# Delta rule: the block-diagonal 128x128 matrices held as packed 64-wide chunks, their products done as 64x64 pairs

## The chip, the core and the metric

One core of a Trainium2 chip runs the whole program. The metric is the device time of one execution in microseconds, the median over several runs.

## What is computed

The program is two transformer blocks over one sequence of 1024 tokens, width 1024: a first block (sparse attention beside a convolution, then an MLP) and a second one (a pooling mixer beside a gated delta rule, then an MLP). The change is in the delta rule of the second block alone. It has 4 heads of 128 channels, chunks of 64 tokens, all in fp32:

```python
diff = gcum[..., :, None] - gcum[..., None, :]
decay_incl = jnp.exp(jnp.where(incl, diff, -jnp.inf))
decay_strict = jnp.where(strict, decay_incl, 0.0)
kb = kh * beta[..., None]
m = jnp.einsum('bhncd,bhnjd->bhncj', kb, kh) * decay_strict       # 64 x 64 per chunk
lhs = jnp.eye(C, dtype=f32) + m
rhs = jnp.concatenate([vh * beta[..., None], kb * jnp.exp(gcum)[..., None]], axis=-1)
sol = lax.linalg.triangular_solve(lhs, rhs, left_side=True, lower=True)
value, k_cumdecay = sol[..., :Dh], sol[..., Dh:]
attn_inner = jnp.einsum('bhncd,bhnjd->bhncj', qh, kh) * decay_incl
...
def step(state, inp):                                             # 16 chunks, one after another
    qd, kc, val, ai, kd, gl = inp
    v_new = val - jnp.einsum('bhcd,bhde->bhce', kc, state)
    o = jnp.einsum('bhcd,bhde->bhce', qd, state) + jnp.einsum('bhcj,bhje->bhce', ai, v_new)
    state = state * jnp.exp(gl)[..., None, None] + jnp.einsum('bhcd,bhce->bhde', kd, v_new)
    return state, o
```

## The kernel before, in words

The delta rule works on 8 tiles of 128 tokens, each two chunks of 64, with the four heads side by side: a matrix per head is 128x128, so a tensor of four is 128 partitions by 512 fp32, one PSUM bank. The matrices that belong to a chunk (m, the inverse of 1 + m, the inner attention) are block-diagonal: two 64x64 blocks in opposite corners, the other two corners zero by the masks `tri`, `strict` and `level[i]`.

The triangular solve is done by doubling. From m, level i's mask cuts out the part b_i that joins blocks of 2^i tokens. t is the inverse so far and u its transpose; level l computes z = b_l-transposed times u, then t - (product of z and t) and u - (product of t and z), l = 1 to 5, where the last needs u alone. Per tile: z1 to z5, t1 to t4, u1 to u5, fourteen groups of four products (one per head). Each fp32 product is two MATMUL instructions of PE, so a group is eight.

Every engine walks one list, `GSTEPS` (line 339), in order. `G_ORDER` gives the steps of a slot: finish_a, chunk_a (0), head_a, level_z 1 to 5, tail_a, chunk_b (0), finish_b, level_tu 1 to 5, chunk_a (1), finish_c, tail_b, head_b, chunk_b (1), head_z. A tile enters every three slots (`SETS = 3`, three sets of buffers `prep[t % 3]`, and PSUM banks 2 * set and 2 * set + 1, called x0 and x1), its step j runs in its slot j, so that three tiles at different depths share each slot. What each step does, with the lines of the profile:

- head_z: VectorE writes z = tri * g (L1798; L1790 for tile 0). head_a: PE multiplies ones by z (L2339, two instructions of 512 columns) into x0 and the gram product of kc with itself into x1 (L2325, the helper `heads`, whose line all group products have); VectorE df (L1801) and the two clamps (L1803, L1804); ScalarE three exponentials (L1200, L1202, L1203); POOL masks e2 (L790).
- head_b: PE kq (L2325); VectorE m from gram, beta and e1 (L1809, four instructions), ait (L1816), u0 (L1818); POOL b0 (L793), t (L795), b1 (L796), qdec (L799); PE turns b0 over (L2330, four transposes).
- level_z and level_tu: PE L2325, ScalarE copies z out of PSUM (L1206), VectorE subtracts t (L1824) and u (L1825), POOL prepares the next b (L808).
- tail_a, tail_b: PE turns kc and vc over, VectorE kbe, kd, vb (L1828, L1831, L1833), PE val and kct (L2325), ScalarE copies them out (L1211, L1213).
- chunk_a, chunk_b: the scan. PE kct and qdec with the state (L2377, L2380), VectorE vnew (L1842) and the decayed state (L1843), PE kd with vnew (L2386), VectorE the new state (L1848), and after the second chunk PE ait with vnew (L2390).
- finish_a to c: ScalarE ot (L1216), VectorE squares and sum, ScalarE root with a table load (L1219), VectorE rec, on and the gated product (L1856, L1858, L1862).

Semaphores `prep_mm`, `prep_dve`, `prep_act` and `prep_pool` count each tile's steps. POOL makes the masks (tri, strict, level) ahead of the list and, after it, splits the weights of the output product. The delta rule begins when the last input product of the second block is done and ends with the copies of h_lo (L1869) for that output product.

Two stretches of the first block are also read below: L2019, `pair_mm`, products of two heads whose operands lie in partitions 0 to 63 and 64 to 127, output to different banks; and L2097, products of 64 output rows that go in turn to PSUM partitions 0 to 63 and 64 to 127 of one bank:

```python
for e in range(2):
    row = slice(HD * e, HD * (e + 1))
    last = mm(ps[:, b[e] + c0 // HALF, 0:cn], q[e][l][row], r[row, c0:c0 + cn], start=(m == 0), stop=(m == 2))
...
last = mm(ps[h % 2 * HD:(h % 2 + 1) * HD, 6, h // 2 * P:(h // 2 + 1) * P],
          vtok[:, bb, kv * HD:(kv + 1) * HD], probT[:, e, bb, :], start=(bb == 0), stop=(bb == t))
```

Of the kernel before, what the change touches and what calls it, by code (L numbers as in the profile page):

```python
# [6 lines left out]
ALU = mybir.AluOpType  # L7
ACT = mybir.ActivationFunctionType
# [60 lines left out]
def build(nc, a, out):  # L69
    with ExitStack() as ctx:  # L70
# [150 lines left out]
        for i, base in enumerate((AH, AH + 32 * K1, AWHI)):  # L221
            names = ["e1", "e2", "egb", "m", "b0", "b1", "z", "t", "u", "kbe", "vb", "ait", "kd", "val", "kct", "qdec"]
            prep.append({nm: at(f"{nm}_{i}", [P, GH, P], F32, base + j * 2 * K1)
                         for j, nm in enumerate(names)})

# [148 lines left out]
        def hb(mask):  # L374

            return mask.unsqueeze(1).to_broadcast([P, GH, P])

# [202 lines left out]
        def _(pool):  # L580
# [204 lines left out]
            g.memset(state, 0.0).then_inc(sem("masks_ready"), 1)  # L785
            for kind, t, l in GSTEPS:
                b = prep[t % SETS]
                if kind == "head_a":
                    pool.wait_ge(prep_sem("act", t), prep_count("act", t, "e2"))
                    g.tensor_tensor(b["e2"], b["e2"], hb(tri), ALU.mult).then_inc(prep_sem("pool", t), 1)  # L790
                if kind == "head_b":
                    pool.wait_ge(prep_sem("dve", t), prep_count("dve", t, "m"))
                    g.tensor_tensor(b["b0"], b["m"], hb(level[0]), ALU.mult).then_inc(prep_sem("pool", t), 1)  # L793
                    pool.wait_ge(prep_sem("pool", t), prep_count("pool", t, "b0"))
                    g.tensor_tensor(b["t"], hb(ident), b["b0"], ALU.subtract).then_inc(prep_sem("pool", t), 1)  # L795
                    g.tensor_tensor(b["b1"], b["m"], hb(level[1]), ALU.mult).then_inc(prep_sem("pool", t), 1)  # L796
                    if t >= SETS:
                        pool.wait_ge(sem("scan_mm"), scan_count("mm", t - SETS, "kq1"))
                    g.tensor_tensor(b["qdec"], qc[:, :, t * P:(t + 1) * P], b["egb"],  # L799
                                    ALU.mult).then_inc(prep_sem("pool", t), 1)  # L800
                if kind == "level_z" and l < 5:

                    if l == 1:
                        pool.wait_ge(prep_sem("mm", t), prep_count("mm", t, "turn"))
                        pool.wait_ge(prep_sem("pool", t), prep_count("pool", t, "t0"))
                    else:
                        pool.wait_ge(prep_sem("mm", t), prep_count("mm", t, f"z{l - 1}"))
                    g.tensor_tensor(b[f"b{(l + 1) % 2}"], b["m"], hb(level[l + 1]), ALU.mult).then_inc(prep_sem("pool", t), 1)  # L808
# [8 lines left out]
        def _(act):  # L817
# [375 lines left out]
            for kind, t, l in GSTEPS:  # L1193
# [10 lines left out]
                if kind == "level_z":  # L1204
                    act.wait_ge(prep_sem("mm", t), prep_count("mm", t, f"z{l}"))
                    s.activation(b["z"], x0, ACT.Copy).then_inc(prep_sem("act", t), 1)  # L1206
# [40 lines left out]
        def _(dve):  # L1247
# [544 lines left out]
            for kind, t, l in GSTEPS:  # L1792
# [12 lines left out]
                if kind == "head_b":  # L1805
                    dve.wait_ge(prep_sem("mm", t), prep_count("mm", t, "gram"))
                    dve.wait_ge(prep_sem("act", t), prep_count("act", t, "e1"))
                    for h in range(GH):
                        last = v.scalar_tensor_tensor(b["m"][:, h, :], x1[:, h, :], gs["beta"][:, t, h:h + 1],  # L1809
                                                      b["e1"][:, h, :], ALU.mult, ALU.mult)  # L1810
# [5 lines left out]
                    v.tensor_tensor(b["ait"], x0, b["e2"], ALU.mult).then_inc(prep_sem("dve", t), 1)  # L1816
                    dve.wait_ge(prep_sem("mm", t), prep_count("mm", t, "turn"))
                    v.tensor_tensor(b["u"], hb(ident), x1, ALU.subtract).then_inc(prep_sem("dve", t), 1)  # L1818
                if kind == "level_tu":
                    dve.wait_ge(prep_sem("mm", t), prep_count("mm", t, f"u{l}"))  # L1820
                    if l < 5:
                        if l == 1:
                            dve.wait_ge(prep_sem("pool", t), prep_count("pool", t, "t0"))
                        v.tensor_tensor(b["t"], b["t"], x0, ALU.subtract).then_inc(prep_sem("dve", t), 1)  # L1824
                    v.tensor_tensor(b["u"], b["u"], x1, ALU.subtract).then_inc(prep_sem("dve", t), 1)  # L1825
# [70 lines left out]
        def _(pe):  # L1896
# [420 lines left out]
            for kind, t, l in GSTEPS:  # L2317
# [9 lines left out]

                def turns(out, src):
# [4 lines left out]
                if kind == "head_a":  # L2333
# [88 lines left out]
```

## Time and profile before

| | us |
|---|---|
| median of 3 runs | 2888.5 (2883.8 to 2890.9) |
| the profiled execution, its own time | 2888.1 |
| its span | 2886.3 |
| busy: PE 93%, VectorE (DVE) 58%, POOL 40%, ScalarE (ACT) 26% | 2687.2, 1686.2, 1153.8, 763.3 |
| mean granted TensorE clock | 0.975 |

PE is TensorE's matmuls, PEld its weight loads. A line of the chain of waits tells where the time that ended last was spent; "x16" after it counts the instructions merged. A line of a timeline has the start, the time from the first start to the last end of the merged instructions, and in brackets the idle time before and what ended it.

### The profile page before, as it was taken

What the parts mean: (1) busy time and instruction counts of PE and PEld (TensorE: products, weight loads), DVE (VectorE), ACT (ScalarE), POOL (GpSimd) and SP (SyncE); (2) the same over time, 40 slices, a digit from 0 to 9 for tenths busy, and PEclk for the clock granted to TensorE, in tenths of its full rate; (3) what the DMA queues carried; (4) which work ended last, traced back from release to release, by engine and by line L of the source; (5) the groups of instructions that cost most, each with busy time, mean ns of one, the idle gap of its engine ahead of it and who ended that gap; (6) DMA issues with size and microseconds to landing.
All of it is one profiled execution on the core that took longest, in us unless ns stands there. A gap on an engine that the chain in (4) does not pass through costs nothing.

```text
span 2886.3 us, 34827 instructions
## 1 busy us (share of the span) xinstructions
PE 2687.2 (93%) x13584; PEld 2207.5 (76%) x13584; DVE 1686.2 (58%) x2150; ACT 763.3 (26%) x1322; POOL 1153.8 (40%) x764
## 2 busy tenths in 40 slices
PE   4999888989999999999999998788799999999998
PEld 4867766777788888888876677777688888888887
DVE  6278988764766567566585772455526334444335
ACT  4235467544321000111032431222214100111002
POOL 2422464544545335345342223333264334334332
PEclk8999999999999999999999999899999999999999
DMA  6201132012311111111122110000221111111111
GB/s 218 66 12 34 38 102 66 8 38 77 106 59 58 38 51 55 40 51 52 43 70 73 37 37 15 1 1 1 93 90 58 42 46 58 39 48 58 36 51 59
DMA packets 142490, 153.35 MB, mean 53 GB/s; under 512 B 7183, under 2 KB 105252, under 8 KB 142374
## 3 DMA queue, kind: packets, MB, share of 16 engines
q1 hardware_dynamic: 137088, 143.97, 15.7%
q10 hardware_dynamic: 5286, 7.79, 0.8%
q8 instruction: 78, 1.28, 0.2%
q14 instruction: 38, 0.31, 0.0%
HBM read 143.35 MB, written 8.39 MB: 53 GB/s over the span
## 4 chain that ended last, share of the span: by engine, by line
PE 77%; DVE 13%; ACT 5%; issue 4%; DMA 1%; POOL 1%; ACTq 0%; SPq 0%; DVEq 0%; POOLq 0%
PE ps L1943 11%; PE ps L1944 11%; PE ps L1928 11%; PE ps L1945 11%; PE ps L1930 11%; PE ps L1929 11%; PE ps L2325 4%; ACT sel_out L960 2%; DVE yt L1765 2%; PE ps L2019 1%; DVE score L1398 1%; DVE yt L1754 1%; DVE best L1396 1%; PE ps L2097 1%; PE ps L1911 1%
## 5 line engine op out<-in xcount | busy, mean ns | idle before, releaser
L1928 PE MATMUL ps<-h_hi,w_hi 128*128 128x512 f32 x1472 | 585.6, 398 | 10.1 <-issue 5.6
L1929 PE MATMUL ps<-h_lo,w_hi 128*128 128x512 f32 x1472 | 575.3, 391 | 0.0
L1930 PE MATMUL ps<-h_hi,w_lo 128*128 128x512 f32 x1472 | 575.1, 391 | 0.0
L707 POOL TENSOR_TENSOR w_hi<-raw,zero 128x1024 fp32r<-128x1024 f32 x128 | 243.7, 1904 | 781.3 <-PE ps L1930 398.4
L1943 PE MATMUL ps<-w_hi,u_hi 128*128 128x512 f32 x1024 | 399.3, 390 | 0.0
L1945 PE MATMUL ps<-w_hi,u_lo 128*128 128x512 f32 x1024 | 399.1, 390 | 0.0
L1944 PE MATMUL ps<-w_lo,u_hi 128*128 128x512 f32 x1024 | 399.1, 390 | 0.0
L1089 ACT ACTIVATE act_r<-ps 128x512 f32<-128x512 f32 x128 | 76.4, 597 | 1131.9 <-PE ps L1930 1131.9
L1649 DVE TENSOR_TENSOR act_r<-act_r 128x512 f32<-128x512 f32 x128 | 165.3, 1292 | 331.0 <-ACT act_r L1089 331.0
L710 POOL TENSOR_TENSOR w_lo<-raw,w_hi 128x1024 fp32r<-128x1024 f32 x128 | 338.1, 2642 | 10.1
L1928 PEld LDWEIGHTS ps<-h_hi,w_hi 128*128 128x128 f32 x1472 | 278.0, 189 | 77.3 <-issue 17.3
L1929 PEld LDWEIGHTS ps<-h_lo,w_hi 128*128 128x128 f32 x1472 | 278.2, 189 | 59.9 <-issue 3.7
L1930 PEld LDWEIGHTS ps<-h_hi,w_lo 128*128 128x128 f32 x1472 | 277.8, 189 | 58.6
L1654 DVE TENSOR_TENSOR u_lo<-act_r,u_hi 128x512 fp32r<-128x512 f32 x128 | 226.8, 1782 | 0.0
L1943 PEld LDWEIGHTS ps<-w_hi,u_hi 128*128 128x128 f32 x1024 | 192.8, 188 | 40.1
L1944 PEld LDWEIGHTS ps<-w_lo,u_hi 128*128 128x128 f32 x1024 | 192.8, 188 | 40.0
L1945 PEld LDWEIGHTS ps<-w_hi,u_lo 128*128 128x128 f32 x1024 | 192.7, 188 | 40.0
L1662 DVE TENSOR_TENSOR x<-x,ps 128x512 f32<-128x512 f32 x128 | 88.0, 687 | 212.2 <-PE ps L1945 212.2
L1943 PE MATMUL ps<-w_hi,h_hi 128*128 128x512 f32 (+2 forms) x512 | 184.3, 360 | 18.3 <-DVE h_lo L1869 6.8
L1944 PE MATMUL ps<-w_lo,h_hi 128*128 128x512 f32 (+2 forms) x512 | 182.5, 357 | 0.0
L1945 PE MATMUL ps<-w_hi,h_lo 128*128 128x512 f32 (+2 forms) x512 | 182.1, 356 | 0.0
L1669 DVE TENSOR_TENSOR x<-x,tmp 128x512 f32<-128x512 f32 x128 | 155.0, 1211 | 4.4
(421 smaller groups left out, 4163.9 us busy)
## 6 DMA issues: line engine op xcount, KB each, us to landing
raw<-in_w_up_dram SPq DMA_DIRECT2D x64, 512.0 KB, 4.0
raw<-in_w_down_dram SPq DMA_DIRECT2D x64, 512.0 KB, 3.2
raw<-in_w_ada_dram SPq DMA_DIRECT2D x48, 512.0 KB, 3.7
raw<-in_w_in_dram SPq DMA_DIRECT2D x32, 512.0 KB, 3.7
raw<-in_w_out_dram SPq DMA_DIRECT2D x32, 512.0 KB, 3.2
x<-in_x_dram SPq DMA_DIRECT2D x12, 512.0 KB, 9.4
x_mid<-x SPq DMA_DIRECT2D x8, 512.0 KB, 5.4
x<-x_mid ACTq DMA_DIRECT2D x8, 512.0 KB, 7.4
```

What stands on the lines that cost most here:

```text
L707: g_.tensor_tensor(w_hi[:, r, :], raw[:, r, :], zero.to_broadcast([P, 1024]), ALU.add).then_inc(sem("w_hi_done"), 1)
L710: g_.tensor_tensor(w_lo[:, r, :], raw[:, r, :], w_hi[:, r, :].bitcast(F32), ALU.subtract).then_inc(sem("split_done"), 1)
L1649: v.tensor_tensor(act_r[:, b % 4, :], act_r[:, b % 4, :], act_r[:, b % 4, :], ALU.mult).then_inc(sem(f"u_sq{k}"), 1)
L1654: v.tensor_tensor(u_lo[c // 4][:, c % 4, :], act_r[:, c % 4, :], u_hi[c // 4][:, c % 4, :].bitcast(F32), ALU.subtract).then_inc(sem(f"u_lo ...
L1669: v.tensor_tensor(x[:, t, cols], x[:, t, cols], tmp2[:, n % 2, :], ALU.add).then_inc(sem(f"x_sum{k}"), 1)
L1928: mm(ps[:, bank, :], wh, h_hi[:, k, cols], start=(k == 0), stop=False)
L1929: mm(ps[:, bank, :], wh, h_lo[:, k, cols], start=False, stop=False)
L1930: last = mm(ps[:, bank, :], wl, h_hi[:, k, cols], start=False, stop=(k == NK - 1))
L1943: mm(o, hi[:, k0 + k, tok], wh, start=(start and k == 0), stop=False)
L1944: mm(o, hi[:, k0 + k, tok], wl, start=False, stop=False)
L1945: last = mm(o, lo[:, k0 + k, tok], wh, start=False, stop=(stop and k == 1))
L2325: last = mm(out[:, h, :], lhs[:, h, :], rhs[:, h, :], start=True, stop=True)
```

## The change

The block-diagonal matrices are packed: e1, e2, m, b0, b1, t, u and z (as zp) become 128 partitions by 4 heads by 64 columns, the upper 64 partitions holding chunk 0's block and the lower ones chunk 1's. The masks get packed copies. gram and kq are made by `column_blocks`, per head two products with all 128 rows of contraction and 64 weight columns and 64 moving columns, whose outputs go to partitions 0 to 63 and 64 to 127 of one bank. z, t, u and the turn of b0 (now a product with the packed identity) are made by `blocks`, per head two 64x64x64 products, chunk 0 from partitions 0 to 63 to partitions 0 to 63 of bank 2 * set, chunk 1 from the other half to the other half of bank 2 * set + 1. Where such a result is read from PSUM it is read by two instructions, one per chunk. The last u (uf) and ait are written to full 128x128 form, whose zero corners POOL clears once per set. The turn now also waits for ait, and tail_a's first turn for u5.

```diff
@@ prep buffers
+            prep[-1]["uf"] = prep[-1]["e2"]
+            for nm, place in (("e1", slot["e1"]), ("e2", slot["e1"] + K1), ("m", slot["m"]), ("t", slot["t"]), ("u", slot["u"]),
+                              ("b0", slot["b0"]), ("b1", slot["b0"] + K1), ("zp", slot["z"])):
+                prep[-1][nm] = at(f"{nm}_half_{i}", [P, GH, CHUNK], F32, place)
+        maskp = at("maskp", [P, 8, CHUNK], F32, AH + 5 * 2 * K1)
+        identp = at("identp", [P, CHUNK], F32, AH + 7 * 2 * K1 + K1)
+        BLOCKS = [slice(CHUNK * c, CHUNK * (c + 1)) for c in range(2)]
+        def chunk_ps(set_, c, part):
+            r = BLOCKS[c]
+            return v3(ps[r, 2 * set_ + c, part * GH * CHUNK:(part + 1) * GH * CHUNK], GH)
+        def packed(b):
+            return v3(ps[:, b, 0:GH * CHUNK], GH)
@@ POOL
+            pool.wait_ge(sem("cm2_full"), cm2_need(len(CH2) - 1))
+            for r in BLOCKS:
+                g.tensor_copy(maskp[r], masks[r, :, r]).then_inc(sem("halves_ready"), 1)
+                g.tensor_copy(identp[r], ident[r, r]).then_inc(sem("halves_ready"), 1)
+            pool.wait_ge(sem("halves_ready"), 4)
...
+                    if t < SETS:
+                        g.memset(b["ait"], 0.0).then_inc(sem("halves_ready"), 1)
+                        g.memset(b["uf"], 0.0).then_inc(sem("halves_ready"), 1)
-                    g.tensor_tensor(b["e2"], b["e2"], hb(tri), ALU.mult).then_inc(prep_sem("pool", t), 1)
+                    g.tensor_tensor(b["e2"], b["e2"], hp(trip), ALU.mult).then_inc(prep_sem("pool", t), 1)
...
@@ ScalarE
-                    s.activation(b["z"], x0, ACT.Copy).then_inc(prep_sem("act", t), 1)
+                    for c, r in enumerate(BLOCKS):
+                        last = s.activation(b["zp"][r], chunk_ps(t % SETS, c, 0), ACT.Copy)
+                    last.then_inc(prep_sem("act", t), 1)
@@ VectorE
-                    v.tensor_tensor(b["e1"], x0, tb(gs["gcum"][:, t, :]), ALU.subtract).then_inc(prep_sem("dve", t), 1)
+                    for r in BLOCKS:
+                        last = v.tensor_tensor(b["e1"][r], x0[r, :, r],
+                                               gs["gcum"][r, t, :].unsqueeze(2).to_broadcast([CHUNK, GH, CHUNK]), ALU.subtract)
...
-                    v.tensor_tensor(b["ait"], x0, b["e2"], ALU.mult).then_inc(prep_sem("dve", t), 1)
+                    dve.wait_ge(sem("halves_ready"), 4 + 2 * min(t + 1, SETS))
+                    for r in BLOCKS:
+                        last = v.tensor_tensor(b["ait"][r, :, r], packed(2 * (t % SETS))[r], b["e2"][r], ALU.mult)
...
-                    v.tensor_tensor(b["u"], hb(ident), x1, ALU.subtract).then_inc(prep_sem("dve", t), 1)
+                    for c, r in enumerate(BLOCKS):
+                        last = v.tensor_tensor(b["u"][r], hp(identp, r), chunk_ps(t % SETS, c, 1), ALU.subtract)
...
-                        v.tensor_tensor(b["t"], b["t"], x0, ALU.subtract).then_inc(prep_sem("dve", t), 1)
+                        for c, r in enumerate(BLOCKS):
+                            last = v.tensor_tensor(b["t"][r], b["t"][r], chunk_ps(t % SETS, c, 1), ALU.subtract)
+                    if l == 5 and t >= SETS:
+                        dve.wait_ge(prep_sem("mm", t - SETS), prep_count("mm", t - SETS, "kct"))
+                    for c, r in enumerate(BLOCKS):
+                        last = v.tensor_tensor(b["uf"][r, :, r] if l == 5 else b["u"][r], b["u"][r], chunk_ps(t % SETS, c, 0),
+                                               ALU.subtract)
@@ PE
+                def column_blocks(b, lhs, rhs, what):
+                    for h in range(GH):
+                        for r in BLOCKS:
+                            last = mm(packed(b)[r, h, :], lhs[:, h, r], rhs[:, h, r], start=True, stop=True)
+                    last.then_inc(prep_sem("mm", t), 1)
+                def blocks(part, lhs, rhs, what):
+                    for h in range(GH):
+                        for c, r in enumerate(BLOCKS):
+                            last = mm(chunk_ps(t % SETS, c, part)[:, h, :], lhs[r, h, :], rhs[r, h, :], start=True, stop=True)
+                    last.then_inc(prep_sem("mm", t), 1)
...
-                    heads(x1, kc[:, :, tok], kc[:, :, tok], "gram")
+                    column_blocks(n0 + 1, kc[:, :, tok], kc[:, :, tok], "gram")
...
-                    heads(x0, kc[:, :, tok], qc[:, :, tok], "kq")
+                    column_blocks(n0, kc[:, :, tok], qc[:, :, tok], "kq")
+                    pe.wait_ge(sem("halves_ready"), 4)
                     pe.wait_ge(prep_sem("pool", t), prep_count("pool", t, "b0"))
-                    turns(x1, b["b0"]).then_inc(prep_sem("mm", t), 1)
+                    pe.wait_ge(prep_sem("dve", t), prep_count("dve", t, "ait"))
+                    blocks(1, b["b0"], hp(identp), "turn")
...
-                    heads(x0, b[f"b{l % 2}"], b["u"], f"z{l}")
+                    blocks(0, b[f"b{l % 2}"], b["u"], f"z{l}")
...
-                        heads(x0, b["z"], b["t"], f"t{l}")
-                    heads(x1, b["t"], b["z"], f"u{l}")
+                        blocks(1, b["zp"], b["t"], f"t{l}")
+                    blocks(0, b["t"], b["zp"], f"u{l}")
                 if kind == "tail_a":
+                    pe.wait_ge(prep_sem("dve", t), prep_count("dve", t, "u5"))
                     turns(x0, kc[:, :, tok]).then_inc(prep_sem("mm", t), 1)
-                    pe.wait_ge(prep_sem("dve", t), prep_count("dve", t, "u5"))
                     turns(x1, vc[:, :, tok]).then_inc(prep_sem("mm", t), 1)
...
-                    heads(x1, b["u"], b["vb"], "val")
-                    heads(x0, b["kbe"], b["u"], "kct")
+                    heads(x1, b["uf"], b["vb"], "val")
+                    heads(x0, b["kbe"], b["uf"], "kct")
```

The other masked products of POOL (b0, t, b1 to b5) and VectorE's m take the packed operands and masks in the same way.

## Rows read from the trace of the kernel before

**Rows 1.** The page of the kernel before, its head.
```profile
span 2886.3 us, 34827 instructions
```

**Rows 2.** Chain that ended last, 1500 to 2200 us: start us, us, what.
```profile
1793.55 2.09 PE ps L2325 x8
1796.31 3.79 PE ps L2325 x16
1801.56 2.06 PE ps L2325 x8
...
1810.15 2.05 PE ps L2339 x2
...
1839.61 1.14 PE ps L2339 x2
...
2006.59 1.51 PE ps L2339 x2
...
2084.17 1.30 DVE h_lo L1869 x2
```

**Rows 3.** The same chain within one steady period, 1937 to 1975 us.
```profile
1939.11 2.06 PE ps L2339 x2
...
1944.53 2.07 PE ps L2325 x16
...
1950.34 0.66 PE ps L2330 x4
1951.00 1.02 PE ps L2377 x8
...
1952.91 2.05 PE ps L2325 x16
...
1956.05 3.77 PE ps L2325 x32
...
1967.17 1.28 ACT L1219
...
1972.90 1.94 PE ps L2339 x2
```

**Rows 4.** Timeline of PE, 655 to 677 us: start us, us, line, xcount.
```profile
660.13 0.40 PE L2123 MATMUL ps<-glu_hi,diag_hi 128*128 128x512 f32 x1
660.36 0.39 PE L2124 MATMUL ps<-glu_lo,diag_hi 128*128 128x512 f32 x1
...
667.13 0.40 PE L2019 MATMUL ps<-k_lo,q_hi 64*128 64x512 f32 x2
667.37 0.39 PE L2019 MATMUL ps<-k_hi,q_lo 64*128 64x512 f32 x2
667.68 1.97 PE L2097 MATMUL ps<-probT,vtok 128*64 128x128 f32 x32
```

**Rows 5.** Timeline of PE's weight loads, 654.3 to 656.2 us.
```profile
655.09 0.19 PEld L2019 LDWEIGHTS ps<-k_hi,q_hi 64*128 64x128 f32 x2
```

**Rows 6.** Groups by line and form, 1785 to 2085 us.
```profile
L1825 DVE TENSOR_TENSOR u<-u,ps 128x512 f32<-128x512 f32 x40 | 26.6, 680 | 0.0
L1206 ACT ACTIVATE z<-ps 128x512 f32<-128x512 f32 x40 | 23.8, 595 | 75.6 <-PE ps L2325 75.6
...
L793 POOL TENSOR_TENSOR b<-m,masks 128x512 f32<-128x512 f32 x8 | 10.1, 1264 | 18.2 <-DVE m L1809 18.2
...
L1809 DVE SCALAR_TENSOR_TENSOR m<-ps,g_beta,e 128x128 f32<-128x128 f32 x32 | 9.0, 344 | 0.8 <-ACT e L1202 0.8
...
L1759 DVE TENSOR_TENSOR zc<-ps,zc 128x1024 f32<-128x1024 f32 x1 | 1.2, 1225 | 0.3 <-ACT zc L1168 0.3
```

**Rows 7.** Stretches: us; busy PE, PEld, DVE, ACT, POOL; PEclk; DMA share, GB/s.
```profile
1805.00:1810.10 5.10, 3.07 (x15) 2.78 (x14) 1.89 (x3) 0.00 (x0) 0.00 (x0) 0.50 0.00 0
1969.30:1972.90 3.60, 0.66 (x4) 0.45 (x5) 3.45 (x6) 0.76 (x1) 0.00 (x0) 1.00 0.00 0
1972.90:1975.00 2.10, 2.10 (x4) 1.06 (x5) 0.12 (x1) 0.00 (x0) 0.00 (x0) 0.53 0.00 0
```

More of the change, by code:

```diff
@@ L224, in build @@
                          for j, nm in enumerate(names)})
+            slot = {nm: base + j * 2 * K1 for j, nm in enumerate(names)}
+            prep[-1]["uf"] = prep[-1]["e2"]
[4 more added lines that the diff above has]
+        identp = at("identp", [P, CHUNK], F32, AH + 7 * 2 * K1 + K1)
+        trip, levelp = maskp[:, 0, :], [maskp[:, 2 + i, :] for i in range(6)]
+        BLOCKS = [slice(CHUNK * c, CHUNK * (c + 1)) for c in range(2)]
         ps = nc.alloc_psum_tensor("ps", [P, 8, HALF], F32).ap()
@@ L376, in hb, with hp @@
             return mask.unsqueeze(1).to_broadcast([P, GH, P])
+        def hp(mask, rows=slice(0, P)):
+            return mask[rows].unsqueeze(1).to_broadcast([rows.stop - rows.start, GH, CHUNK])
+        def chunk_ps(set_, c, part):
[3 more added lines that the diff above has]
+            return v3(ps[:, b, 0:GH * CHUNK], GH)
         def tb(col):
@@ L807, in _ @@
                         pool.wait_ge(prep_sem("mm", t), prep_count("mm", t, f"z{l - 1}"))
-                    g.tensor_tensor(b[f"b{(l + 1) % 2}"], b["m"], hb(level[l + 1]), ALU.mult).then_inc(prep_sem("pool", t), 1)
+                    g.tensor_tensor(b[f"b{(l + 1) % 2}"], b["m"], hp(levelp[l + 1]), ALU.mult).then_inc(prep_sem("pool", t), 1)
             pool.wait_ge(sem("scan_mm"), scan_count("mm", LAST_AT_W, "ai"))
@@ L1800, in _ @@
                     dve.wait_ge(prep_sem("mm", t), prep_count("mm", t, "gb"))
-                    v.tensor_tensor(b["e1"], x0, tb(gs["gcum"][:, t, :]), ALU.subtract).then_inc(prep_sem("dve", t), 1)
+                    for r in BLOCKS:
+                        last = v.tensor_tensor(b["e1"][r], x0[r, :, r],
+                                               gs["gcum"][r, t, :].unsqueeze(2).to_broadcast([CHUNK, GH, CHUNK]), ALU.subtract)
+                    last.then_inc(prep_sem("dve", t), 1)
                     dve.wait_ge(prep_sem("dve", t), prep_count("dve", t, "df"))
@@ L1808, in _ @@
                     for h in range(GH):
-                        last = v.scalar_tensor_tensor(b["m"][:, h, :], x1[:, h, :], gs["beta"][:, t, h:h + 1],
+                        last = v.scalar_tensor_tensor(b["m"][:, h, :], packed(2 * (t % SETS) + 1)[:, h, :], gs["beta"][:, t, h:h + 1],
                                                       b["e1"][:, h, :], ALU.mult, ALU.mult)
@@ L1815, in _ @@
                         dve.wait_ge(sem("scan_mm"), scan_count("mm", t - SETS, "ai"))
-                    v.tensor_tensor(b["ait"], x0, b["e2"], ALU.mult).then_inc(prep_sem("dve", t), 1)
+                    dve.wait_ge(sem("halves_ready"), 4 + 2 * min(t + 1, SETS))
+                    for r in BLOCKS:
+                        last = v.tensor_tensor(b["ait"][r, :, r], packed(2 * (t % SETS))[r], b["e2"][r], ALU.mult)
+                    last.then_inc(prep_sem("dve", t), 1)
                     dve.wait_ge(prep_sem("mm", t), prep_count("mm", t, "turn"))
-                    v.tensor_tensor(b["u"], hb(ident), x1, ALU.subtract).then_inc(prep_sem("dve", t), 1)
+                    for c, r in enumerate(BLOCKS):
+                        last = v.tensor_tensor(b["u"][r], hp(identp, r), chunk_ps(t % SETS, c, 1), ALU.subtract)
+                    last.then_inc(prep_sem("dve", t), 1)
                 if kind == "level_tu":
@@ L1823, in _ @@
                             dve.wait_ge(prep_sem("pool", t), prep_count("pool", t, "t0"))
-                        v.tensor_tensor(b["t"], b["t"], x0, ALU.subtract).then_inc(prep_sem("dve", t), 1)
-                    v.tensor_tensor(b["u"], b["u"], x1, ALU.subtract).then_inc(prep_sem("dve", t), 1)
+                        for c, r in enumerate(BLOCKS):
+                            last = v.tensor_tensor(b["t"][r], b["t"][r], chunk_ps(t % SETS, c, 1), ALU.subtract)
+                        last.then_inc(prep_sem("dve", t), 1)
+                    if l == 5 and t >= SETS:
[3 more added lines that the diff above has]
+                                               ALU.subtract)
+                    last.then_inc(prep_sem("dve", t), 1)
                 if kind == "tail_a":
```

6 lines of the change are left out of this document (3 added, 3 removed).

## The prediction

> **What bounds the kernel now.** I began with the page's first part: the span is 2886.3 us [rows 1]. The change touches only the delta rule, so I looked for it in the chain of waits over 1500 to 2200 us. Eight tiles of 128 tokens enter one after another, each with the product of ones and z (L2339); the next phase begins with h_lo (L1869) at 2084.17 [rows 2]. The tiles' starts give the stages: fill, in which tile 0 and then tile 1 enter (1810.15), up to tile 2's start at 1839.61; five steady periods, 1839.61 to 2006.59, 33.4 us each; and the drain, 2006.59 to 2084.17, 77.6 us. Together that is a tenth of the kernel, and all that the change can gain is in there.
>
> In one steady period [rows 3], 33.8 us from 1939.11 to 1972.90, I see three parts. **A**, from L2339 to the turn of b0 at 1950.34 (11.2 us), goes through VectorE's and ScalarE's head work until t3, u3 start at 1944.53, 5.4 us in, and then through a queue of five products on TensorE. **B**, the turn to about 1964.7, is almost bare TensorE: the scan's products, z1 and z4 (x16, 2.05 us), then t1, u1, t4, u4 (x32, 3.77 us). **C**, to 1972.90, waits for ScalarE (table load and root at 1967.17) and then VectorE; TensorE hardly matters. So TensorE's product groups are worth their price in B, part of it in A, nearly nothing in C. From x16 in 2.05 and x32 in 3.77, 16 instructions cost 1.72 us, 0.11 us each: a group of four heads, eight instructions since each fp32 product is two, costs 0.88 us, and its result comes 0.2 us after its last start.
>
> **The change, part by part.**
>
> *The products.* gram, kq and turn, five z, four t and five u become 64x64 halves: 16 instructions a group in place of eight (the turn's were four). Whether it pays hangs on the rate. Four bounds: (1) A matmul with 64 rows of contraction alternating between the two row halves: the second product costs nothing. Pairs of 64x512 start 0.24 us apart (667.13 and 667.37) and single 128x512 ones 0.23 us (660.13, 660.36) [rows 4]; their two weight loads run side by side too, x2 in 0.19 us [rows 5]. (2) Outputs alternating between column halves: L2097, 64 weight columns and 128 moving ones, x32 in 1.97 us, 0.055 us each [rows 4], half of the 0.11 us of full products. (3) With the moving columns halved as well, 0.055 becomes 0.0275 us: a group costs 0.44 us. (4) The other end is 0.055 us, the fastest rate of weight load plus matmul that a row shows: 0.88 us, no gain at all. For the products in opposite corners (turn, z, t, u) I take 0.44, since rows 4 and 5 show both matmuls and loads of different row halves together; for gram and kq, whose pairs share all rows, I take L2097's rate, 0.88.
>
> *Changes of shape.* From one form to another there is a small gap: L2019's last pair starts at 667.37 and L2097 only at 667.68, 0.31 us later in place of 0.23 [rows 4]. I take 0.09 us a change, about eight more of them a period, half on the path; between 0 and 0.15.
>
> *Packed element work.* A VectorE operation from PSUM takes 1225 ns at 1024 elements and 680 at 512 [rows 6]: 1.06 ns an element, so 256 take 0.41 us, and the second of two, whose fixed part overlaps, starts about 0.33 later (no less than the 0.27 of its elements). Where a copy is split by chunk (df, ait, u0, t, u) two halves take about 0.75 in place of 0.68: +0.07 each. They can't be under half of 0.68 nor over twice it. ScalarE's z, 595 ns, becomes two halves of 0.39, 0.32 apart: +0.1. Operations truly halved gain: two clamps and two exponentials -0.13 to -0.2 each, m (four of 344 ns) -0.25, POOL's products 1264 ns to about 0.73 (between 0.63 and 1.26).
>
> *Part A.* df +0.07, clamps -0.26, the ScalarE run e1, e2, z3 -0.3: t3 starts at 4.9 in place of 5.4 (if none of the halves is cheaper than the whole, at 5.4 again). Then on TensorE t3 and u3 0.88, change 0.09, val and kct 1.76, change 0.09, kq 0.88, result 0.2: 8.8. Here the added wait bites: the turn now waits for ait, which needs kq; queued behind the turn stand chunk_a, z1 and z4. ait's halves end at 9.55, the turn starts at 9.6 (11.2 before). The other leg, t3/u3 on VectorE (1.4), m (0.85), b0 (0.8), ends at 9.0, so ait is late next. A gains 1.6 us.
>
> *Part B.* The turn 0.66 becomes 0.44 and a change; chunk_a keeps its 1.9; z1 and z4 2.05 become 0.97: -1.0. t1, u1, t4, u4 3.77 become 1.76 and 0.2: -1.8. The rest (chunk_a, its vnew wait, kdv, ai) stays. ScalarE's z4 is ready just when t4 comes. B gains 2.9.
>
> *Part C.* z2 and z5 come 0.4 to 0.5 sooner, t2, u2, u5 are six halves: +0.2. The table load, root, rec, on, gated and z stay. C gains 0.3. tail_a's kc turn now waits for u5 of its tile, which VectorE finished in the part before: nothing.
>
> *Sum.* 4.8 us off 33.8 is 29.0 a period. The 33.8 holds a slow start: TensorE's granted clock is 0.53 right after the idle stretch (1972.9 to 1975.0) [rows 7], 1.2 instead of 2.4 GHz, while the period that begins at 1839.61 has L2339 in 1.14 us [rows 2]. With longer idle in C I expect that in all: 5 x (33.4 - 29.0) = 22. *Fill*: tile 0 runs alone, and at half clock: one level took 1801.56 - 1793.55 = 8.0 us [rows 2], z 2.09 and t, u 3.79 of it. Halved products leave 1.1 and 2.0, the split copies cost 0.2: 2.7 a level, two levels 5.4, and 2.4 in tile 0's head (POOL's masking of e2 and b0, then t and b1 against the turn, 1.7; clamps and exponentials 0.7): 7.8. Tile 1's 29.5 us hold three slots of the same kind, partly at full clock: 7, between 4 and 9. *Drain*: one period's 4.8, then 1.35 and 1.2 where z, t, u are still in the way of chunk_a: 7.3; the last 20 us are scan alone, nothing. *POOL's new copies* of the masks and memsets sit between the last input product and e2's mask, under L2339 and VectorE's head: nothing; uncovered they cost up to 2 us once. Total 22 + 7.8 + 7 + 7.3 = 44 us. The profiled execution took 2888.1 us, 1.8 around its span and 0.4 below the median of 2888.5. 2888.1 - 44 = 2844.
>
> **Rivals.** *1. Halves do not overlap, or issue limits them:* 0.055 us each, a group 0.88, the turn dearer by 0.3. For it: no row shows a weight load and matmul pair under 0.055 us. Against: rows 5. Then A gains 0.8 and loses 0.3 at the turn, changes and split copies take the rest, the fill keeps 2: about 2885, from 2881 to 2890. Chance 0.20. The Trainium skill, page "TensorE: Matmul & The Clock Gate", section "Wait — 56ns, not 53.3ns?", says that the sequencer, without hardware decode, spends about 62 ns on each matmul, which binds once array work is shorter. By it a group would be 0.99 us and the time some 8 us above this rival's. L2097's 32 in a row at 55 ns speak against it, but no run shows narrower ones; of the 0.20, 0.03 is for it.
>
> *2. The clock stays low; the slower end.* TensorE's work a period falls from 25 to about 18 us and its idle share grows. Rows 7 show both sides: from 1805 to 1810 busy for 3.07 of 5.10 us the clock stayed at 0.50, while it was 1.00 in 1969.3 to 1972.9 after a dense stretch, with 0.66 busy of 3.6, and fell right after. Place: parts A and B. Price: at 1.2 GHz A costs 3.6 us more (t3, u3, val, kct, kq), B 9.5, C 0.5: 13.6 a period, 42.6 in place of 29.0. Over five periods, less fill and drain, that is about 2915. It decides against the change once more than a third of each period (4.8 of 13.6) is at 1.2 GHz. Against: B is dense in the new schedule too, and density has lifted the clock. Chance 0.10, two thirds of it slower than before.
>
> *3. More gain:* kq overlaps too, the changes of shape are free and the low start shrinks: another 1 to 2 us a period and 4 in the fill, 2830. Chance 0.10.
>
> **How the numbers follow.** Forecast 0.60, with its own range 2832 to 2866 (group price 0.40 to 0.60, fill 4 to 9). Measured no-change for this kernel is about 0.3%, 8.7 us. Faster: 0.60, 0.10, part of rival 2 (0.03) and of rival 1 (0.04): 0.77. Same: most of rival 1, 0.15. Slower: 0.07 of rival 2 and the rest of rival 1: 0.08. The range reaches 2824 (rival 3 and a cheaper fill) to 2882, leaving out most of rivals 1 and 2.
>
> **What would show it.** L2339's starts about 29 us apart; t, u, z groups x16 in about 0.6 us; the chain in B still TensorE; the turn released by ait; tile 1's start to tile 2's about 22 us. Groups at 0.9 to 1.0 us show rival 1; granted clock 0.5 in B shows rival 2. I am wrong if the periods stay at 33 with short groups: then a wait that I took as covered has the place of the products.

## The result, and the profile after

The changed kernel takes 2871.95 us, the median of 4 runs (2870.19 to 2875.62), against 2889.08 us for the kernel before in the same comparison: 0.9945 of it, 95% interval 0.9928 to 0.9963. It is faster by 17 us. The forecast was 2844 us, 44 us less than the profiled execution, with a range of 2824 to 2882.

The page of the kernel after, its head:

```profile
span 2868.5 us, 37231 instructions
...
PE 2649.3 (92%) x14704; PEld 2162.1 (75%) x14704; DVE 1699.3 (59%) x2246; ACT 766.0 (27%) x1362; POOL 1125.3 (39%) x774
```

The span is 17.8 us shorter than that of [rows 1], though TensorE has 1120 matmuls more. The product of ones and z, with which each tile starts, is now L2397, and the 64x64 products are L2383. The chain of waits over 1750 to 2100 us (start us, us, what) has the tiles' starts and the fill:

```profile
1784.93 1.11 PE ps L2397 x2
...
1791.94 0.86 PE ps L2383 x16
1793.65 2.00 PE ps L2383 x32
1797.55 1.13 PE ps L2383 x16
...
1804.14 2.06 PE ps L2397 x2
...
1828.85 1.12 PE ps L2397 x2
...
1989.93 1.70 PE ps L2397 x2
...
2065.31 1.30 DVE h_lo L1915 x2
```

Beside [rows 2]: in the kernel before tile 0 started here:

```profile
1784.33 1.10 PE L2339 MATMUL ps<-z,ones 128*128 128x512 f32 x2 [0.98 <-DVE z L1790]
```

The delta rule, from tile 0's product of ones and z to h_lo, took 2084.17 - 1784.33 = 299.8 us and takes 2065.31 - 1784.93 = 280.4 us, so 19.4 us went here. What the three stages gave, in us:

| | before | forecast | after |
|---|---|---|---|
| fill, tile 0's start to tile 2's | 55.3 | 40.5 | 43.9 |
| five periods, us each | 33.4 | 29.0 | 32.2 |
| drain, tile 7's start to h_lo | 77.6 | 70.3 | 75.4 |

The loss against the forecast is above all in the steady periods: 22 us were expected of them and 6 came. The chain within one of them, 1957.24 to 1989.93, to be laid beside [rows 3]:

```profile
1957.24 2.05 PE ps L2397 x2
...
1962.47 0.69 DVE kbe L1874
...
1964.42 2.05 PE ps L2371 x16
1966.47 0.64 PE ps L2377 x16
...
1968.13 0.68 PE ps L2383 x16
...
1970.71 1.08 PE ps L2383 x32
...
1972.87 1.10 PE ps L2383 x32
...
1974.00 0.41 DVE t_half L1864
...
1974.42 0.42 DVE t_half L1864
...
1974.88 0.41 DVE u_half L1869
...
1975.31 0.42 DVE u_half L1869
...
1977.49 0.62 DVE vnew L1888
...
1980.61 1.93 PE ps L2383 x32
...
1983.34 1.28 ACT L1250
...
1985.79 0.41 DVE t_half L1864
...
1989.93 1.70 PE ps L2397 x2
```

The lines to see are the pairs of L1864 and L1869. After the products of the four groups (x32, 1.10 us at the end, in place of the 3.77 us of [rows 3]) the chain no longer goes on with chunk_a on TensorE. It goes through eight halves on VectorE, from 1974.00 until vnew at 1977.49, and through six more before the next tile, from 1985.79. A half is 0.41 us long and the next starts 0.42 to 0.46 us after it: no overlap at all. The second thing is the start of the period. kbe begins 5.2 us after L2397, and val and kct (L2371) start only when vb is done, 7.2 us after it. The clock there and in part C, by the same columns as [rows 7]:

```profile
1957.20:1962.40 5.20, 5.16 (x39) 3.45 (x40) 1.43 (x4) 1.97 (x5) 0.73 (x2) 0.50 0.01 3
1979.90:1983.40 3.50, 3.49 (x53) 3.08 (x53) 1.51 (x3) 2.16 (x6) 0.00 (x0) 0.52 0.00 0
```

The first 5.2 us of the period are at 0.50, and z2 and z5 in part C (0.52) are at the low clock too, x32 in 1.93 us. Before, the first stretch (1939.1 to 1944.3) had 0.69. Not every period is like this one. Over the five, the starts of L2397 are 32.1, 31.1, 32.0, 33.2 and 32.7 us apart; z2 and z5 are at the low clock in the first, fourth and fifth, and take 1.15 us in the other two. The mean granted clock of the five is 0.88, against 0.97 before.

Groups by line and form over 1785 to 2070 us, to be read beside [rows 6]:

```profile
L2383 PE MATMUL ps<-u_half,b_half 64*64 64x64 f32 x640 | 30.8, 257 | 7.1 <-DVE u_half L1869 5.1 <-DVE u_half L1856 2.1
...
L2383 PE MATMUL ps<-identp,b_half 64*64 64x64 f32 x128 | 5.5, 222 | 10.8 <-DVE ait L1852 8.2 <-POOL b_half L822 2.5
```

The 640 instructions of the z groups have 257 ns each in flight, against 299 for the full products before; what fell is the distance between them, for in the chain above two groups, 32 instructions, last 1.08 us. The turn (identp, b_half) waited 10.8 us in all over eight tiles, 8.2 of them for ait.

### The profile page after: what moved, and what is told of

Read it like the earlier page. It is cut to its first block, busy times and chain, and to the rows that moved or that the text cites. A ratio compares the mean times of both kernels' runs of the same rounds, so it can differ in the third digit from the quotient of the medians.

```text
span 2868.5 us, 37231 instructions
## 1 busy us (share of the span) xinstructions
PE 2649.3 (92%) x14704; PEld 2162.1 (75%) x14704; DVE 1699.3 (59%) x2246; ACT 766.0 (27%) x1362; POOL 1125.3 (39%) x774
## 4 chain that ended last, share of the span: by engine, by line
PE 76%; DVE 14%; ACT 5%; issue 4%; DMA 1%; POOL 0%; ACTq 0%; SPq 0%; DVEq 0%; POOLq 0%
PE ps L1989 11%; PE ps L1991 11%; PE ps L1990 11%; PE ps L1974 11%; PE ps L1976 11%; PE ps L1975 11%; ACT sel_out L989 2%; PE ps L2383 2%; DVE yt L1796 2%; PE ps L2065 2%; DVE score L1429 1%; DVE yt L1785 1%; DVE best L1427 1%; PE ps L2143 1%; DVE u_half L1869 1%
## 5 line engine op out<-in xcount | busy, mean ns | idle before, releaser
L1974 PE MATMUL ps<-h_hi,w_hi 128*128 128x512 f32 x1472 | 585.5, 398 | 10.1 <-issue 5.6
L731 POOL TENSOR_TENSOR w_lo<-raw,w_hi 128x1024 fp32r<-128x1024 f32 x128 | 338.1, 2642 | 10.1
```

The lines of the kernel that those rows point to most:

```text
L731: g_.tensor_tensor(w_lo[:, r, :], raw[:, r, :], w_hi[:, r, :].bitcast(F32), ALU.subtract).then_inc(sem("split_done"), 1)
L1974: mm(ps[:, bank, :], wh, h_hi[:, k, cols], start=(k == 0), stop=False)
```

## The experiments

Times below are medians of four or more runs. The kernel before was run again in each comparison, with medians of 2887.3 to 2890.2 us, and each ratio is to its own. "Stretch" is tile 0's start to h_lo in the profiled execution; tile 0 starts anywhere from 1782.75 to 1787.48 us in these executions, so stretches and periods are compared beside the medians.

| kernel | us | ratio to before, interval | stretch | period |
|---|---|---|---|---|
| before | 2889 | | 299.8 | 33.4 |
| after | 2872.0 | 0.9945 (0.9928 to 0.9963) | 280.4 | 32.2 |
| whole_reads | 2843.7 | 0.9833 (0.9816 to 0.9849) | 258.4 | 29.0 |
| chunk_order | 2866.6 | 0.9911 (0.9894 to 0.9927) | 276.8 | 30.9 |
| warm_clock | 2866.9 | 0.9922 (0.9906 to 0.9939) | 276.7 | 31.0 |
| no_pairs | 2894.3 | 1.0014 (1.0004 to 1.0024) | 303.0 | 33.7 |
| whole_warm | 2844.4 | 0.9851 (0.9834 to 0.9867) | 256.5 | 28.2 |
| whole_early_z | 2818.2 | 0.9760 (0.9744 to 0.9776) | 228.6 | 25.2 |
| before_early_z | 2871.7 | 0.9951 (0.9934 to 0.9968) | 282.7 | 30.7 |
| one_bank | 2842.8 | 0.9844 (0.9828 to 0.9861) | 256.7 | 29.0 |
| whole_short_warm | 2841.0 | 0.9829 (0.9812 to 0.9845) | 249.5 | 27.5 |
| best_no_ait_wait | 2813.2 | 0.9732 (0.9715 to 0.9748) | 224.8 | 24.0 |

**whole_reads: one suspected cost taken away.** The theory after the first look: the split reads on VectorE took back what the products gave. The rival: the clock did.

```diff
+        ORDER = [(0, 0), (2, 1), (1, 0), (3, 1), (0, 1), (2, 0), (1, 1), (3, 0)]
+        def head_ps(set_, h, c, part):      # heads 0, 1 in the first bank, 2, 3 in the second
+            col = part * GH * CHUNK + h % 2 * CHUNK
+            return ps[BLOCKS[c], 2 * set_ + h // 2, col:col + CHUNK]
-                            last = v.tensor_tensor(b["t"][r], b["t"][r], chunk_ps(t % SETS, c, 1), ALU.subtract)
+                        v.tensor_tensor(two(b["t"]), two(b["t"]), whole(t % SETS, 1), ALU.subtract)
```

> The changed kernel with the chunks' results laid out so that VectorE and ScalarE read them whole: heads 0 and 1 of both chunks in the first bank of the set, heads 2 and 3 in the second, order of the pairs such that the two at work write different banks. z, u0, t and u up to level 4 are then one instruction of 128x256 each in place of two of 64x256. Theory (the split reads ate the gain: two halves follow each other 0.43 us apart, so t1, u1, t4, u4 take 3.5 us on the path, t2, u2, u5 2.6 us): consecutive whole ones 0.33 us apart, t1, u1, t4, u4 in 1.5 us, a steady period 3 us shorter (29 in place of 32.2), 2846 us in all, 2840 to 2855. Rival (the low clock is what ate it): the period shortens by less than 1 us, 2864 to 2872. Rival (TensorE is slower with banks shared by the two chunks): x16 groups above 0.7 us.

Measured: 2843.7 us, a period of 29.0. The timeline of VectorE in part B, and one line of TensorE in part C:

```profile
1952.62 0.42 DVE L1873 TENSOR_TENSOR t_half<-t_half,ps 128x256 f32<-128x256 f32 x1 [0.41 <-PE ps L2393]
...
1952.96 0.41 DVE L1877 TENSOR_TENSOR u_half<-u_half,ps 128x256 f32<-128x256 f32 x1
...
1953.56 0.42 DVE L1873 TENSOR_TENSOR t_half<-t_half,ps 128x256 f32<-128x256 f32 x1 [0.18 <-PE ps L2393]
1953.90 0.41 DVE L1877 TENSOR_TENSOR u_half<-u_half,ps 128x256 f32<-128x256 f32 x1
...
1955.43 0.69 DVE L1898 TENSOR_TENSOR vnew<-val,ps 64x512 f32<-64x512 f32 x1 [1.12 <-PE ps L2450]
...
1958.35 1.15 PE L2393 MATMUL ps<-u_half,b_half 64*64 64x64 f32 x32
```

t and u are one instruction each, 0.34 us apart, and vnew starts at 1955.43, released by TensorE's chunk_a: part B is bare TensorE again. The last line is z2 and z5 in part C: x32 in 1.15 us, full clock, and so in all five periods. The theory holds in size, 28 us where 26 were expected, and both rivals fall as the main cause. ScalarE has a share in it: from the start of z2 to the table load of L1219's counterpart it is 1.60 us here (1958.35 to 1959.95) and 2.30 us in the kernel after where the clock is full (1883.17 to 1885.47), since four halves of z are copied in 1.56 us and two whole ones in 0.85.

**chunk_order: why halves are dear.** The same halves in another order.

```diff
                     for c, r in enumerate(BLOCKS):
-                        last = v.tensor_tensor(b["t"][r], b["t"][r], chunk_ps(t % SETS, c, 1), ALU.subtract)
-                    for c, r in enumerate(BLOCKS):
+                        if l < 5:
+                            last_t = v.tensor_tensor(b["t"][r], b["t"][r], chunk_ps(t % SETS, c, 1), ALU.subtract)
                         last = v.tensor_tensor(b["uf"][r, :, r] if l == 5 else b["u"][r], b["u"][r], chunk_ps(t % SETS, c, 0),
```

> The changed kernel with VectorE's halves of a level ordered t, u of chunk 0, then t, u of chunk 1, in place of t of both, u of both. Theory (two instructions lose their overlap when the first partition changes from 0 to 64 or back; with the same first partition they overlap by about 0.1 us, as vnew after u of the second chunk does): the four take 1.55 in place of 1.75 us, two of three starts change to one of three, a period 0.4 to 0.6 us shorter, 2868 us. Rival (short instructions cannot overlap, whatever their partitions): four still 1.75 us, 2872.

```profile
1968.92 0.41 DVE L1866 TENSOR_TENSOR t_half<-t_half,ps 64x256 f32<-64x256 f32 x1 [0.40 <-PE ps L2383]
1969.25 0.41 DVE L1869 TENSOR_TENSOR u_half<-u_half,ps 64x256 f32<-64x256 f32 x1
1969.67 0.42 DVE L1866 TENSOR_TENSOR t_half<-t_half,ps 64x256 f32<-64x256 f32 x1
1970.02 0.42 DVE L1869 TENSOR_TENSOR u_half<-u_half,ps 64x256 f32<-64x256 f32 x1
```

t and u of chunk 0 start 0.33 us apart, u of chunk 0 and t of chunk 1 0.42, then 0.35. So it isn't the shortness. Two instructions that start at the same partition overlap by 0.08 us; where the first partition changes, they don't. The Trainium skill, page "VectorE: DVE Perf Modes", section "Two Vector instructions with no wait between them", has this as a rule, which it calls a model: an instruction whose input or output starts in another group of 32 partitions than the last one in that memory is held until every earlier one has finished. The traces agree: held halves start 0.42 us after neighbours that are 0.41 long, and here every second one is free of it. By that rule every half of a period but the first of each run would have been priced at its full length ahead of the run, for each starts on other partitions than the one ahead of it. The kernel before had the sign of it too, in vnew and the decay of the state behind it. vnew of chunk 0 starts at partition 0 and that of chunk 1 at partition 64, the state always at 0:

```profile
1952.92 0.68 DVE L1842 TENSOR_TENSOR vnew<-val,ps 64x512 f32<-64x512 f32 x1 [1.20 <-PE ps L2380]
1953.53 1.10 DVE L1843 TENSOR_TENSOR state<-state,egb 128x512 f32<-128x512 f32 x1
...
1961.74 0.69 DVE L1842 TENSOR_TENSOR vnew<-val,ps 64x512 f32<-64x512 f32 x1 [0.61 <-PE ps L2380]
1962.46 0.69 DVE L1843 TENSOR_TENSOR state<-state,egb 128x512 f32<-128x512 f32 x1
```

The starts are 0.61 us apart for chunk 0 and 0.72 for chunk 1.

The median is 5.4 us less than after, where 4 were expected. A period is 1.3 us shorter, more than the 0.6 expected, and what is over goes with the clock: TensorE's wait for vnew1 (vnew of chunk 1) is 0.96 us here and 1.38 us in the kernel after, and z2 and z5 behind it are at the full clock in all five periods here, at the low one in three of five there. That the longer stall brings the clock down is suggested by this, not isolated.

**warm_clock: the other suspect.**

```diff
+                    pe.wait_ge(sem("scan_dve"), scan_count("dve", t, "snew1"))
+                    for i in range(6):
+                        mm(bank(6)[:, i % GH, :], ones, ident, start=True, stop=True)
                     pe.wait_ge(sem("scan_dve"), scan_count("dve", t, "on"))
                     turns(bank(7), ot).then_inc(sem("scan_mm"), 1)
+                    for i in range(14):
+                        mm(bank(6)[:, i % GH, :], ones, ident, start=True, stop=True)
```

> The changed kernel with idle products of ones and the identity added on TensorE into bank 6, which is free there: 6 before the wait for on, 14 after the turn of ot, about 4 us of work in the stretch in which TensorE waits for VectorE before each tile. Nothing of the result is changed. Theory (the granted clock falls in that stretch and part A then runs at 1.2 GHz up to kbe): granted clock 1.00 over the first 5 us of a period, L2339's counterpart 1.1 us in place of 2.05, kbe starts 3.2 us after it in place of 5.2, the period 1.5 to 2 us shorter, 2858 us, 2854 to 2864. Rival (part A is bound by the element work anyway): kbe sooner, val no sooner, 2870 to 2873.

```profile
1955.30:1960.50 5.20, 4.40 (x74) 3.25 (x74) 3.32 (x7) 1.97 (x5) 1.42 (x2) 1.00 0.00 0
```

The clock is 1.00 over the first 5.2 us, and a period is 31.0 in place of 32.2, 1.2 less where 1.5 to 2 were expected. The median fell by 5 us, not 14: it lies outside the expected 2854 to 2864, and the intervals of the two ratios overlap, so the gain is read from the stretch, 3.6 us shorter. Part A, from L2397 to the turn, is 8.9 us in place of 10.9, as the theory has it; but the wait for vnew1 is still there, z2 and z5 still run at the low clock in four of the five periods, part C is half a microsecond longer, and the drain 2.2 us. The clock is a real cost, but not the main one.

**no_pairs: does the overlap of corners exist?** One line swapped, `for c` outside `for h`.

> The changed kernel with the 64x64 products ordered by chunk: all four heads of chunk 0, then all of chunk 1, so that neighbours use the same corner of the array. Theory (pairs in opposite corners overlap, 0.028 us an instruction): a group x16 goes from 0.64 to about 1.05 us at full clock, the two z groups x32 from 1.08 to 1.9, a period 1.5 to 2.5 us longer, 2885 to 2892 us. Rival (the rate is set by something else than corners): unchanged, 2872.

The timeline of TensorE:

```profile
1965.57 1.54 PE L2383 MATMUL ps<-u_half,b_half 64*64 64x64 f32 x32
...
1985.59 0.93 PE L2383 MATMUL ps<-identp,b_half 64*64 64x64 f32 x16 [1.05 <-DVE ait L1852]
```

Two z groups last 1.54 us in place of 1.15, the turn 0.93 in place of 0.68. The expected 1.9 and 1.05 were too much, and so was the rate of rival 1 in the prediction, but the total, 2894.3, is beyond the expected 2885 to 2892: 22 us slower than after, and nothing of the change's gain is left. The pairs are what makes it pay.

**whole_warm and whole_short_warm: both costs at once.** The idle products on whole_reads, first with 14 after the turn, then with 8.

> Whole reads (as in whole_reads, 2843.7 us) and the idle products that keep TensorE's clock up before each tile (as in warm_clock, which took 1.5 us off a period of the changed kernel). If the two costs are separate: period 29.0 to 27.5, 2836 us, 2833 to 2840. If the split reads hid the clock's cost, or the other way round: 2842 to 2845.

> whole_warm with 8 idle products in place of 14 after the turn of ot, since the 14 stood on the chain of waits before the product of ones and z there. Theory (the clock costs 1.5 us a period also with whole reads): 27.3 to 27.9 us a period, 2836 us, 2833 to 2841. Rival: 28.5 to 29.0, 2842 to 2846.

whole_warm missed: 2844.4. Its chain of waits shows why:

```profile
1931.92 1.54 PE ps L2466 x12
...
1933.97 3.13 PE ps L2470 x28
1937.10 0.88 PE ps L2407 x2
```

With whole reads the idle stretch is 1 us shorter, and the 14 idle products (L2470, 3.13 us) stand on the chain ahead of L2407. With 8 a period is 27.5 us, 1.5 less than whole_reads, as the theory has it, and 2841.0 us is at the edge of the expected 2833 to 2841. The medians differ by only 2.7 us, although the stretch is 8.9 us shorter. In the two profiled executions tile 0 starts 4.0 us later and the time is 4.5 us less, which leaves 0.5 us lost behind h_lo; and the profiled execution of whole_reads was its slowest, 1.9 us above its median, that of this kernel 0.1 above. Why tile 0 starts later in one execution than in another is open.

**one_bank: is "each chunk in its own bank" needed?**

```diff
-            return ps[BLOCKS[c], 2 * set_ + h // 2, col:col + CHUNK]
+            return ps[BLOCKS[c], 2 * set_ + part, h * CHUNK:(h + 1) * CHUNK]
```

> Whole reads with all eight blocks of a group in one bank: chunk 0 in partitions 0 to 63, chunk 1 in partitions 64 to 127, pairs in the plain order, so that the two products at work write the same bank in different partitions. Theory (only the partitions matter): as whole_reads, x16 at 0.64 us, 2844 us, 2841 to 2847. Rival, a rule of the Trainium skill, page TensorEngine Tiling (Array Packing), Gotcha 1: row tiles cannot access one bank simultaneously; the pairs would be serial, x16 at 0.9 us or more, 2860 us or more.

```profile
1954.14 0.68 PE L2391 MATMUL ps<-t_half,zp_half 64*64 64x64 f32 x16
1954.65 0.63 PE L2391 MATMUL ps<-zp_half,t_half 64*64 64x64 f32 x16
```

The groups start 0.46 to 0.51 us apart, as in whole_reads, and the time is the same, though the pairs are back in the plain order: so it wasn't their order that helped in whole_reads. The rule of the Trainium skill, page "TensorEngine Tiling (Array Packing)", section "Gotcha 1: PSUM Pressure", that the expectation took as its rival doesn't hold here, for products in opposite corners, whose outputs lie in different partitions. So the layout of the change was not needed for the pairs, and it is what forced the reads to be split.

**whole_early_z, before_early_z: the chain of part C.** One entry of the list of steps moved, on whole_reads and on the kernel before.

```diff
-        G_ORDER += [("chunk_b", 7, 0), ("finish_b", 8, 0)]
+        G_ORDER += [("chunk_b", 7, 0), ("head_z", -1, 0), ("finish_b", 8, 0)]
```

> Whole reads, and head_z (z = tri * g, which needs only what is long there) moved in the order of steps from the end of the slot to before finish_b, where VectorE waits for ScalarE's table load and root. Theory (part C is a chain of VectorE: on, t, u, u5, gated, z, and then TensorE's product of ones and z): that product starts right after the turn of ot, df 2.3 us sooner, a period 29.0 to 26.8, 2828 us, 2823 to 2833. Rival (part A is bound elsewhere, by ktp and kbe): a period 28 to 29, 2838 to 2844.

> The kernel before with head_z moved in the same way and nothing else. Theory: part C is the same chain there, so it gains 2 us a period, 2874 us, 2870 to 2880: then the move is independent of the packed products. Rival (before, TensorE and not VectorE bounds the start of a tile): 2884 to 2890.

The chain is as the theory has it in both, and the size in the second: 16 us less than before (15 expected). A period of before_early_z is 30.7: this one moved entry is worth as much as the whole change. On whole_reads it gives 25 us where 16 were expected, and 2818.2 is below the expected 2823 to 2833. Part C is 6.85 us there in place of 9.26, near the 2.3 expected, and part A about 8.9 in place of 10.3, which the expectation didn't have. Granted clock over the five periods of whole_early_z, by the columns of [rows 7]:

```profile
1816.50:1942.30 125.80, 105.55 (x1793) 92.12 (x1791) 82.39 (x181) 38.88 (x70) 36.64 (x45) 1.00 0.01 2
```

With L2407's counterpart right after the turn of ot, TensorE's long idle stretch is gone, and with it the fall of the clock, which whole_short_warm had priced at 1.5 us a period. This fits part A's gain.

**best_no_ait_wait: the added wait.** One bank, early z, and no wait of the turn for ait.

```diff
                     pe.wait_ge(prep_sem("pool", t), prep_count("pool", t, "b0"))
-                    pe.wait_ge(prep_sem("dve", t), prep_count("dve", t, "ait"))
                     blocks(1, b["b0"], hp(identp), "turn")
```

In the change's layout the wait keeps TensorE from writing the bank that VectorE still reads. Here the turn writes the set's second bank, which ait doesn't read, so what made it wait is gone.

> One bank for both chunks (as one_bank), early z (as whole_early_z, 2818.2 us), and the turn's wait for ait taken away: its result then goes to the set's second bank, which VectorE's ait does not read, so that the reason for the wait is gone with the wait. Theory (the added wait is late next, as the prediction has it): the turn starts right after kq, 0.9 us sooner, a period 0.5 to 1 us shorter, 2811 us, 2808 to 2816. Rival (b0 or u0 is late just behind it): less than 0.2 us a period, 2816 to 2820.

```profile
1944.75 0.62 PE ps L2385 x16
1945.37 0.61 PE ps L2391 x16
1945.98 1.02 PE ps L2444 x8
```

kq (L2385), the turn (L2391) and chunk_a (L2444) follow one another without a gap. A period is 1.1 us shorter than in whole_early_z (0.5 to 1 expected), and 2813.2 us is inside the expected 2808 to 2816. This version beats both kernels: 2.7% less than before and, by the two ratios, 2.1% less than after.

## Why the prediction was wrong

It had the sign, and a range that held the time, but the size was over twice the measured one. The main step that failed is the price of the split copies, in what they cost on VectorE and, through TensorE's stall, very likely in the clock; a second one is the path through part A. By its own steps:

- **The rate of the halves: right.** Forecast was 0.0275 us an instruction where pairs share nothing; groups of 16 start 0.47 us apart, 0.029. For gram and kq it took 0.055 from L2097, which has 128 moving columns where they have 64, and kq came at about 0.03, as rival 3 had it. no_pairs shows that the overlap is the cause. Rival 1 falls.
- **The split copies: the step that failed.** "Where a copy is split by chunk (df, ait, u0, t, u) two halves take about 0.75 in place of 0.68: +0.07 each", the second starting "about 0.33 later". That gave the halves of one operation an overlap which only instructions that start at the same partition have (chunk_order). Measured start to start: 0.42 to 0.46. The comparison was wrong too: in a run of operations a whole one costs 0.60 and not its length of 0.68, as the chain before shows with L1825 x2 in 1.20. Two halves cost 0.88, so a split costs 0.28 in place of 0.07, seven times a period on VectorE (fourteen halves): 1.5 us. And the packed tensor read whole would have cost 0.34 (whole_reads): a half of the partitions is no cheaper than all of them, 0.41 us long either way.
- **Part B, forecast 9.2 us** (the turn to the second kdv): 1968.13 to 1978.16 is 10.0, before 12.2. Of the 0.8 missing 0.6 is four splits: by the forecast u4's last half and TensorE's chunk_a ended together; with the true price VectorE is 0.6 us behind and becomes the bound (TensorE's wait for vnew1 is 1.38 us, and 0.78 before and in whole_reads, where B is 9.4).
- **Part C, forecast 10.1** (to the next L2397): 11.8, before 10.4. Of the 1.7 missing 0.7 is the clock: z2 and z5, and the end of L2450 ahead of them, are at 1.2 GHz, and in the two periods in which they aren't C is 11.06. Three splits are 0.6. ScalarE's z has a part in the rest: its halves follow each other 0.39 us apart and not 0.32. After the stall of 1.38 us in B the clock was low in three of five periods; with a stall of 0.96 (chunk_order) or 0.78 (whole_reads) in none, so this too very likely comes from the split reads.
- **Part A, forecast 9.6:** 10.9, before 11.2. "ait is late next" was true (the turn's row above), but another leg came before it, from kc's turn through kbe, kd and vb to val, which the forecast had at nothing. It let val start 5.9 us after the tile's start; vb releases it at 7.2. Even in the kernel before vb ended at 6.8 (kbe starts at 4.9), hidden behind TensorE's t3 and u3. Halving these uncovers it, and gram, z3 and kc's turn at 1.2 GHz push kbe to 5.2. warm_clock, with the clock up, has kbe at 2.9 and A at 8.9 us. The forecast's reading of A before was off too: there the chain leaves TensorE at u3 and reaches the turn through u (1947.22), m and b0, and val, kct and kq, the rest of the "queue of five products", aren't on it. Rival 2 had the clock's mechanism: the mean clock of 0.88 over the five periods means about a quarter of their time at 1.2 GHz (an estimate from the two levels), against the third at which it would decide. Its 2915 us is also 3 more than 2844 and five times its 13.6 give.
- **The sum.** A, B and C miss by 1.3, 0.8 and 1.7 in this period. Over the five they are 10.5, 10.0 and 11.7 and miss by 0.9, 0.8 and 1.6, together 3.2 us a period, 16 us of the 25 us that are missing in the stretch. The 0.9 of A isn't the split reads' (whole_reads takes 0.2 of it away); of the rest, 0.6 in B, 0.6 in C and, if the clock falls by the stall, 0.6 more in C are. whole_reads then lands on the forecast's 29.0 us and 2844 us, but partly by luck: its parts are 10.3, 9.4 and 9.3, so A is 0.7 us longer, B 0.2 longer and C 0.8 shorter than forecast, since t2 and u2 are whole there, 0.33 us apart in place of the forecast's two halves, and ScalarE's z is whole; and its fill and drain miss in opposite directions.
- **Fill, forecast 14.8 us less:** 11.4, and 17.7 with whole reads. A level alone took 1797.55 - 1791.94 = 5.6 us against a forecast 5.3: the same split term.
- **Drain, forecast 7.3 less:** 2.2, and 1.8 with whole reads. So it isn't the reads. From 2019.61 on the chain goes through kbe, val and the scan and hardly through the halved products, which the forecast had only for the last 20 us, and the scan now runs beside POOL's split of the output weights. The timeline of the kernel after:

```profile
2032.41 2.34 POOL L771 TENSOR_TENSOR w_lo<-raw,w_hi 128x1024 fp32r<-128x1024 f32 x1
2032.71 2.60 DVE L1889 TENSOR_TENSOR state<-state,egb 128x512 f32<-128x512 f32 x1
```

The decay of the state takes 2.60 us beside POOL's L771, in place of 0.69, and it is on the chain: 1.9 us of the 5.1 missing. Before, one such instruction met it too (2.04 us at 2053.42), off the chain. What the rest of the drain's loss is was not tested.
- **POOL's copies and memsets:** forecast nothing. e2's mask starts 0.07 us after its exponential, so nothing of them is uncovered. But tile 0's z on VectorE, beside POOL's copies, takes 1.08 us in place of 0.69: 0.4 us, once.

## What to carry to other kernels

When products get cheaper, price what reads them, by the distance from start to start in a busy queue and not by the length of one instruction; an instruction cut into two partition halves costs more than twice the whole one, here 0.88 us in place of 0.34 for 128x256. Choose the layout of the results in PSUM by how they are read: here one bank for both chunks served the pairs as well and left the reads whole. Look for what an in-order list keeps waiting for no reason: one moved entry was worth as much as the whole change.

## What the runs showed that was not expected

- VectorE's neighbours overlap by about 0.08 us when they start at the same partition and not when the start changes: 0.33 us against 0.42 to 0.46 between halves of 256 elements (chunk_order); between vnew and the state after it 0.61 against 0.72 (before).
- A VectorE subtraction of 64x256 and one of 128x256 are both 0.41 us long (after, whole_reads).
- ScalarE may have the same: two exponentials of 128x256 start 0.32 us apart, the halves of z, 64x256, 0.39. But these differ in more than their partitions, and no run isolates it.
- Two 64x64 products in opposite corners overlap fully also when they write one bank (one_bank).
- TensorE's wait for vnew1 of 1.38 us was followed by the low clock in three of the five periods of after and four of the five of warm_clock; waits of 0.78 (whole_reads), 0.96 (chunk_order) and 1.16 us (no_pairs) never were. What decides it among equal waits is open.
- Without pairs, 16 halves took 0.93 us and not the 1.05 expected, 0.047 us an instruction.
